# One layer of a hybrid trunk on one core: norm and gate stage in one block, the attention loop of TensorE written out, the order of two emptyings changed in the final stage

## The chip, the core and the metric

The kernel runs on one core of a Trainium2 chip. The metric is the device time of one execution in microseconds (us); a time given for a kernel is the median of several executions.

## What is computed

One decoder layer runs for a prompt of 1024 tokens and a sample group of 8 x 8 tokens, 1088 tokens (`NT`) in all, in float32. Cut to what matters here:

```
xn = RMSNorm_pre(x);  z = xn @ w_in                      (1024 -> 13312 columns)
A: dilated windowed softmax attention, 3 groups x 4 heads -> 512
B: HGRN2, 8 heads, 128 x 128 state                        -> 1024
C: causal pooling over 2, 4, 8, 16 positions              -> 512
gates = sigmoid(mg)                                       (mg: 3 x 1024 columns of z)
merged = gates_0*(y_a @ w_br_a) + gates_1*(y_b @ w_br_b) + gates_2*(y_c @ w_br_c)
x_next = x + RMSNorm_post(merged @ w_out)
```

## The kernel before

Each matrix is held as a sum of a rounded part ("hi", type fp32r) and a remainder ("lo"), and a product is three matmuls: hi x hi, lo x hi, hi x lo. Features lie on the partitions and tokens on the free axis; a projection of 128 columns (a "unit", `Conveyor.project`, L233 for its matmuls) runs in three chunks of 384, 384 and 320 tokens, one PSUM bank each. `Conveyor.load` (L200, SyncE's queue) brings raw weights, `Conveyor.split` (L207, L209, GpSimd) makes their hi and lo parts, `Conveyor.empty` (L246, L247, ScalarE) copies a bank out and frees it. Every engine has its own list of instructions in program order, written by hand, with semaphores between them; there is no planner. A stage is a block (`nc.Block`), and engines meet at its end.

The stages in order: `norm_phase` (normalise, transpose through TensorE, split x into `x_hi` and `x_lo`; the first unit runs in between), `gate_phase`, `attention_phase`, `hgrn_phase`, `pool_phase`, `final_phase`.

**Gate stage** (L478 to L763). Unit 1 is projected first, then ten pairs (`PAIRS`) of 128 gate columns go by a seven-product scheme: the 1024 features and the 1088 tokens are halved, and seven products r = 0 to 6 of 512 features by 544 tokens replace eight (L639, each in two pieces j of 272 tokens and 24 matmuls). Products 0, 3 and 5 take a plain quarter of x; products 1, 2, 4 and 6 take a combination of quarters: t1 = x12 - x11, t2 = x22 - t1, t3 = x22 - x12 and t4 = x21 - t2, where x11 to x22 are hi plus lo of a quarter. VectorE makes the quarters' sums and most differences (L705, L731 to L738), GpSimd two of these (L583, L586), ScalarE rounds them (`round_t`, L655) and the remainders are taken by VectorE (L710) and once by GpSimd (L592). The weights need four sums per pair (`w_sums`, VectorE, L727), and GpSimd splits the seven weight blocks of a pair (L578, L580) into a ring of four slots. Products run in the order 0 to 6. ScalarE copies products 0, 1 and 2 out (L652), VectorE adds them to products 3, 4 and 5 (L748, L754, L760), ScalarE takes the sigmoid and issues the store (L689, L693). Unit 1's banks are emptied by ScalarE between the roundings, and TensorE's first product waits until all three are empty.

**Attention stage**. TensorE runs four heads in a loop, `with pe.Fori(0, AH) as h` (L1833); so do the other engines, each with a loop of its own. A head ends with the next head's unit 0 and begins with its unit 1.

**Final stage** (L765 to L1172). Eight units of branch B (`U_B + t`) run with `y_hi`, `y_lo`; meanwhile the eight 128-row tiles of branches A and C are loaded one per t (`ac_stage`), rounded by ScalarE (`split_ac`, L1019) and their remainders taken by VectorE (L1096); TensorE waits for all eight (`acl_ready`) before the A and C units. Then t = 0 to 7 runs a unit of A (`u_a(t)`) and one of C (`u_c(t)`), four feature tiles each. ScalarE's list per t is:

```
for t in range(KO):
    if t > 0:
        act.wait_ge(ml_ready, t)          # y_lo of t-1 is made (VectorE L1116)
    empty u_a(t) into pb[0], c = 0, 1, 2
    if t < LAST:
        empty u_c(t) into pb[1], c = 0, 1, 2
        act.wait_ge(m_ready, t + 1)       # merged tile t (VectorE L1111, L1114)
        y_hi[t] = round(pb[1])            # L1047
```

A unit's chunk c can start only when the unit before has had its bank c emptied, so `u_c(t)` waits for the emptying of `u_a(t)`.

## Time and profile before

| | us |
|---|---|
| median of 3 runs (lowest, highest) | 1954.68 (1951.04, 1956.36) |
| the profiled execution | 1951.46 |
| its span, first to last instruction | 1949.6 |
| TensorE busy in it | 1868.6 (96%) |
| VectorE, ScalarE, GpSimd busy | 825.0, 385.1, 546.6 |
| mean granted TensorE clock | 0.988 of full speed |

PE is TensorE's matmul side, DVE VectorE, ACT ScalarE, POOL GpSimd, SP SyncE. Ends of matmuls are modelled, so their durations overlap; the spacing of the starts is the rate. "[14.47 <-X]" means 14.47 us idle before the instruction, ended by X. Times in the rows count from the span's start.

### The profile page before, as it was taken

To read this page: it belongs to the slowest core of one execution; us is meant where nothing else is said; L and a number is where in the kernel's file an instruction comes from. 1 tells how busy PE (TensorE), PEld (TensorE's weight loads), DVE (VectorE), ACT (ScalarE), POOL (GpSimd) and SP (SyncE) were. 2 spreads that over 40 slices of the span, in tenths; PEclk is the share of its full clock that TensorE was granted. 3 is DMA by queue.
4 is the path that set the end of the run, shared out by engine and by line. 5 is a ranking of instruction groups with operands and counts; after the bars stand their busy time and mean duration, and the time that the engine had idled before them with its cause. 6 is when DMAs were issued, how large, how long until landed. Compare 5 with 4: busy or idle time off the path is not lost. (4 is left out here: it accounts for less than half of the span.)

```text
span 1949.6 us, 34834 instructions
## 1 busy us (share of the span) xinstructions
PE 1868.6 (96%) x13888; PEld 1793.8 (92%) x13888; DVE 825.0 (42%) x1380; ACT 385.1 (20%) x922; POOL 546.6 (28%) x371
## 2 busy tenths in 40 slices
PE   7599999999999999999999999999999998989898
PEld 6599999989998999999999999999999998988897
DVE  7532321231232133113255675566466384446623
ACT  5222221310211221022011111101101112222321
POOL 2676662211221221221222221222212232344200
PEclk9799999999999999999999999999999999999999
DMA  5132324142233324314212112112202224555522
GB/s 163 55 111 92 112 91 124 52 107 76 72 63 112 95 53 105 103 48 97 84 45 67 35 53 67 44 54 67 67 22 68 67 91 164 181 196 175 158 96 87
DMA packets 245179, 176.31 MB, mean 90 GB/s; under 512 B 35789, under 2 KB 226637, under 8 KB 245068
## 3 DMA queue, kind: packets, MB, share of 16 engines
q1 hardware_dynamic: 205036, 132.51, 23.9%
q10 hardware_dynamic: 40032, 42.15, 6.3%
q8 instruction: 90, 1.47, 0.3%
q14 instruction: 21, 0.17, 0.0%
HBM read 131.83 MB, written 42.79 MB: 90 GB/s over the span
## 5 line engine op out<-in xcount | busy, mean ns | idle before, releaser
L233 PE MATMUL psum<-x_hi,w_hi 128*128 128x384 f32 (+1 forms) x2208 | 732.4, 336 | 24.6 <-ACT c_ext L247 10.4
L233 PE MATMUL psum<-x_lo,w_hi 128*128 128x384 f32 (+1 forms) x2208 | 714.9, 328 | 7.0 <-issue 7.0
L233 PEld LDWEIGHTS psum<-x_hi,w_hi 128*128 128x128 f32 x2208 | 418.3, 189 | 47.9 <-issue 33.8
L207 POOL CAST w_hi<-w_raw 128x1024 fp32r<-128x1024 f32 (+1 forms) x108 | 114.9, 1064 | 1187.9 <-PE psum L233 915.1
L233 PEld LDWEIGHTS psum<-x_lo,w_hi 128*128 128x128 f32 x2208 | 418.9, 190 | 0.0
L233 PE MATMUL psum<-x_hi,w_lo 128*128 128x384 f32 (+1 forms) x2208 | 412.2, 326 | 0.0
L233 PEld LDWEIGHTS psum<-x_hi,w_lo 128*128 128x128 f32 x2208 | 370.7, 188 | 0.0
L209 POOL TENSOR_TENSOR w_lo<-w_raw,w_hi 128x1024 fp32r<-128x1024 f32 (+1 forms) x108 | 258.5, 2393 | 8.6
L2044 ACT ACTIVATE a_feature<-psum 128x384 f32<-128x384 f32 (+1 forms) x100 | 45.2, 452 | 368.3 <-PE psum L233 363.4
L2156 DVE TENSOR_TENSOR a_prob<-psum,band 128x128 f32<-128x128 f32 (+1 forms) x64 | 21.5, 378 | 216.9 <-PE psum L1850 215.6
L639 PE MATMUL psum<-g_sum_hi,w_hi 128*128 128x272 f32 x320 | 85.6, 294 | 7.6 <-POOL w_hi L578 7.6
L639 PE MATMUL psum<-g_sum_lo,w_hi 128*128 128x272 f32 x320 | 85.0, 293 | 0.0
L639 PE MATMUL psum<-x_hi,w_hi 128*128 128x272 f32 x240 | 63.3, 291 | 14.5 <-ACT a_feature L247 14.5
L580 POOL TENSOR_TENSOR w_lo<-g_tmp,w_hi 128x512 fp32r<-128x512 f32 x55 | 74.2, 1350 | 4.4
L639 PEld LDWEIGHTS psum<-g_sum_hi,w_hi 128*128 128x128 f32 x320 | 62.2, 194 | 7.9 <-issue 7.9
L233 PE MATMUL psum<-m_y_hi,w_hi 128*128 128x384 f32 (+1 forms) x192 | 62.2, 328 | 2.4 <-DVE m_y_lo L1088 2.4
L1362 PEld LDWEIGHTS psum<-b_q_decayed,b_k_decayed 128*64 128x64 f32 x1584 | 51.3, 138 | 13.0 <-issue 8.4
L639 PE MATMUL psum<-x_lo,w_hi 128*128 128x272 f32 x240 | 63.2, 291 | 0.0
L233 PE MATMUL psum<-m_y_lo,w_hi 128*128 128x384 f32 (+1 forms) x192 | 62.4, 330 | 0.0
L639 PEld LDWEIGHTS psum<-g_sum_lo,w_hi 128*128 128x128 f32 x320 | 62.0, 194 | 0.0
L748 DVE TENSOR_TENSOR g_tmp<-psum,g_tmp 128x272 f32<-128x272 f32 x20 | 8.8, 442 | 124.3 <-PE psum L639 124.3
L639 PEld LDWEIGHTS psum<-x_hi,w_hi 128*128 128x128 f32 x240 | 46.2, 193 | 14.7 <-ACT a_feature L247 14.7
(275 smaller groups left out, 2582.5 us busy)
## 6 DMA issues: line engine op xcount, KB each, us to landing
w_raw<-in_w_in SPq DMA_DIRECT2D x94, 512.0 KB, 3.9
gate_rows<-g_tmp ACTq DMA_DIRECT2D x20, 544.0 KB, 2.9
s_cached<-in_cache_kv_w SPq DMA_DIRECT2D x128, 64.0 KB, 2.5
s_cached<-in_cache_kv_w SPq DMA_DIRECT2D x64, 128.0 KB, 2.4
spare<-branch_outputs SPq DMA_DIRECT2D x13, 544.0 KB, 6.2
a_feature<-group_weights SPq DMA_DIRECT2D x12, 512.0 KB, 5.0
c_gate<-gate_rows SPq DMA_DIRECT2D x11, 544.0 KB, 3.6
c_gate_raw<-gate_rows SPq DMA_DIRECT2D x11, 544.0 KB, 4.0
```

The lines of the kernel that those rows point to most:

```text
L207: pool.tensor_copy(w_hi[:, s, 0:nko, :], w_raw[:, s, 0:nko, :]).then_inc(self.hi_ready, 1)
L209: pool.tensor_tensor(w_lo[:, s, 0:nko, :], w_raw[:, s, 0:nko, :], w_hi[:, s, 0:nko, :].bitcast(F32), ALU.subtract)\
L233: mm = pe.matmul(psum[:, c, 0:n], w[:, s, k, :], x[:, k, t0:t0 + n], start=step is first, stop=step is last)
L580: pool.tensor_tensor(ring(w_lo, m), source(n, r), ring(w_hi, m).bitcast(F32), ALU.subtract)\
L639: mm = pe.matmul(bank(n, r, j), w[:, a.start, b.start + k, :], piece(x, j)[:, k, :], start=(r in (0, 1, 3) and w is w_hi and x is hi and k ...
L748: dve.tensor_tensor(outs[0][:, j * N:(j + 1) * N], bank(n, 3, j), kept1[j], ALU.add)\
L1362: mm = pe.matmul(bank[r:r + HP, b * wq:(b + 1) * wq], kr[:, t0 + r:t0 + r + HP], second(q[:, t0 + r:t0 + r + HP], n), start=True, stop=True)
L2044: ins = act.activation(by_class(DST[j][:, 0:SEQ], g)[:, :, t0 // STEP[g]:end // STEP[g]], psum[:, c, 0:end - t0].rearrange("p (m r) -> p r ...
L2156: ins = dve.tensor_tensor(prob[:, a:a + w], ps_, mask, ALU.add)
```

## The change

The norm stage and the gate stage become one block. The sums and differences of x, of the first pair's weights and their remainders all go to VectorE, the roundings of the first pair's weights to ScalarE; GpSimd splits weights from the second pair on. The first pair's raw weights are loaded as soon as unit 1's are split. The products run in the order 0, 3, 1, 2, 5, 4, 6, so that two plain ones come first; within a product the matmuls with the remainder of x come last. Scratch tiles share the memory of the x rows, `g_pre` and `q0`. In attention TensorE's loop over the heads is a Python loop, so its instructions are written four times; the other engines keep their loops. In the final stage two tiles of A and C are brought at each of the first four t, and ScalarE empties `u_a(t + 1)` right after it rounds tile t, without waiting for that tile's remainder.

```diff
-        def norm_phase(then, q0):
-
-
+        def norm_and_gate_phase(first, then, q0):
...
+            ORDER = (0, 3, 1, 2, 5, 4, 6)
+            SHIFT = 66
...
+                area = sb("x_rows", (P, (TILES + 1) * D), F32, scope)
+                xt = area[:, :].rearrange("p (t d) -> p t d", d=D)
...
+                junk = q0[:, 0:D]
...
+                FULLS = {"x12": 1, "x11": 2, "t1": 3, "x22": 4, "t2": 5, "t3": 6, "x21": 7, "t4": 8}
...
+                def slot(m):
+
+                    return m % 4 if m < SHIFT else (m + 2) % 4
...
+                        sp.wait_ge(cv.split_done, 2 * SLOTS)
+                        for n in range(PAIRS):
+                            if n == 1:
+                                sp.wait_ge(t_full, FULLS["t4"])
+                            if n > 1:
+                                weights_ready(sp, 7 * (n - 1) - 1)
...
+                        for n in range(1, PAIRS):
+                            for r in ORDER:
+                                m = place(n, r)
+                                source_ready(pool, n, r)
+                                slot_free(pool, m)
+                                pool.tensor_copy(ring(w_hi, m), source(n, r)).then_inc(p_hi_ready, 1)
+                                high_ready(pool, m)
+                                pool.tensor_tensor(ring(w_lo, m), source(n, r), ring(w_hi, m).bitcast(F32), ALU.subtract)\
+                                    .then_inc(p_ready, 1)
...
+                        for n in range(PAIRS):
+                            for r in ORDER:
+                                m = place(n, r)
+                                hi, lo, ready = moving(r)
+                                if n == 0 and r == 0:
+                                    cv.emptied(pe, 1)
...
+                                    if r == 0 and n > 1:
+                                        pe.wait_ge(copied, 8 * (n - 2) + 7 + j)
+                                    elif r == 3 and n > 0:
+                                        pe.wait_ge(summed, 6 * (n - 1) + 1 + j)
+                                    elif r == 1 and n > 0:
+                                        pe.wait_ge(summed, 6 * (n - 1) + 3 + j)
+                                    elif r == 2:
+                                        pe.wait_ge(copied, 8 * n + 1 + j)
+                                    elif r == 5:
+                                        pe.wait_ge(copied, 8 * n + 3 + j)
+                                    elif r == 4:
+                                        pe.wait_ge(copied, 8 * n + 5 + j)
+                                    elif r == 6:
+                                        pe.wait_ge(summed, 6 * n + 5 + j)
...
+                                    steps = [(w_hi, hi, k) for k in range(HK)] + [(w_lo, hi, k) for k in range(HK)]
+                                    steps += [(w_hi, lo, k) for k in range(HK)]
...
+                        def round_t(n, full, src):
+                            act.wait_ge(t_full, FULLS[full])
+                            act.activation(t_hi[n][:, :, :], src, ACT.Copy).then_inc(t_hi_ready, 1)
+
+                        def round_w(r):
+                            m = place(0, r)
+                            source_ready(act, 0, r)
+                            slot_free(act, m)
+                            act.activation(ring(w_hi, m), source(0, r), ACT.Copy).then_inc(first_hi_ready, 1)
...
+                        cv.emptied(act, 0, 1)
+                        act.activation(q0[:, 0:t0], q0[:, 0:t0], ACT.Sigmoid).then_inc(closed, 1)
+                        cv.empty(act, 0, NCH - 1, q0, ACT.Sigmoid)
+                        round_w(0)
+                        round_w(3)
+                        cv.emptied(act, 0)
+                        act.wait_ge(closed, 1)
+                        act.dma_start(gates_d[0], q0[:, :]).then_inc(first_out, 16)
+                        act.wait_ge(first_out, 16)
+                        cv.empty(act, 1, 0, q0, ACT.Sigmoid)
+                        round_t(0, "t1", tmp[1])
+                        cv.empty(act, 1, 1, q0, ACT.Sigmoid)
+                        cv.empty(act, 1, 2, q0, ACT.Sigmoid)
+                        round_w(1)
+                        round_w(2)
+                        cv.emptied(act, 1)
+                        act.dma_start(gates_d[1], q0[:, :]).then_inc(first_out, 16)
+                        round_t(1, "t2", tmp[3])
+                        for j in range(2):
+                            copy(kept1[j], 0, 0, j)
+                        round_w(5)
+                        round_t(2, "t3", tmp[0])
+                        round_w(4)
+                        for j in range(2):
+                            copy(kept5[j], 0, 1, j)
+                        round_w(6)
+                        round_t(3, "t4", tmp[3])
...
+                        def whole(name, dst, a, b):
+                            dve.tensor_tensor(dst, quarter(x_hi, a, b).bitcast(F32), quarter(x_lo, a, b).bitcast(F32),
+                                              ALU.add).then_inc(t_full, 1)
+
+                        def differ(name, dst, x, y, needs):
+                            dve.wait_ge(t_full, FULLS[needs])
+                            dve.tensor_tensor(dst, x, y, ALU.subtract).then_inc(t_full, 1)
+
+                        def low(n, src):
+                            dve.wait_ge(t_hi_ready, n + 1)
+                            dve.tensor_tensor(t_lo[n][:, :, :], src, t_hi[n][:, :, :].bitcast(F32), ALU.subtract)\
+                                .then_inc(t_ready[n], 1)
+
+                        def low_w(r):
+                            m = place(0, r)
+                            high_ready(dve, m)
+                            dve.tensor_tensor(ring(w_lo, m), source(0, r), ring(w_hi, m).bitcast(F32), ALU.subtract)\
+                                .then_inc(first_ready, 1)
...
+                        w_sums(0, (0, 1))
+                        dve.wait_ge(xt_done, 2 * (TILES + 1))
+                        dve.wait_ge(banks_free, 2 * (TILES + 1))
+                        whole("x12", tmp[0], 0, 1)
+                        whole("x11", tmp[1], 0, 0)
+                        w_sums(0, (2,))
+                        differ("t1", tmp[1], tmp[0], tmp[1], "x11")
+                        low_w(0)
+                        low_w(3)
+                        whole("x22", tmp[2], 1, 1)
+                        low(0, tmp[1])
+                        differ("t2", tmp[3], tmp[2], tmp[1], "x22")
+                        low_w(1)
+                        low_w(2)
+                        differ("t3", tmp[0], tmp[2], tmp[0], "x22")
+                        low(1, tmp[3])
+                        dve.wait_ge(t_full, FULLS["t3"])
+                        dve.wait_ge(t_full, FULLS["t2"])
+                        whole("x21", tmp[2], 1, 0)
+                        w_sums(0, (3,))
+                        low_w(5)
+                        dve.wait_ge(t_ready[1], 1)
+                        differ("t4", tmp[3], tmp[2], tmp[3], "x21")
+                        low(2, tmp[0])
+                        low_w(4)
+                        low(3, tmp[3])
+                        low_w(6)
+                        dve.wait_ge(t_ready[2], 1)
...
+                        for n in range(PAIRS):
+                            if n > 0:
+                                dve.wait_ge(out[0], 16 * n)
+                            for j in range(2):
+                                product_done(dve, n, 3, j)
+                                dve.wait_ge(copied, 8 * n + 1 + j)
+                                dve.tensor_tensor(outs[0][:, j * N:(j + 1) * N], bank(n, 3, j), kept1[j], ALU.add)\
+                                    .then_inc(summed, 1)
+                            if n + 1 < PAIRS and n > 0:
+                                w_sums(n + 1)
+                            for j in range(2):
+                                product_done(dve, n, 5, j)
+                                dve.wait_ge(copied, 8 * n + 5 + j)
+                                dve.tensor_tensor(outs[0][:, HN + j * N:HN + (j + 1) * N], bank(n, 5, j), kept2[j], ALU.add)\
+                                    .then_inc(summed, 1)
+                            if n > 0:
+                                dve.wait_ge(out[1], 16 * n)
+                            for j in range(2):
+                                product_done(dve, n, 4, j)
+                                dve.tensor_tensor(outs[1][:, HN + j * N:HN + (j + 1) * N], bank(n, 4, j), kept5[j], ALU.add)\
+                                    .then_inc(summed, 1)
+                            if n == 0:
+                                w_sums(1)
...
                         weights(U_B + 1)
                         sp.wait_ge(yl_ready, KO)
                         for t in range(KO):
-                            if t >= 3:
-                                sp.wait_ge(acl_ready, t - 2)
-                            sp.dma_start(ac_stage[t % 3][:, :], y_d[Y_A + t]).then_inc(ac_in[t % 3], 16)
+                            for k in (2 * t, 2 * t + 1) if t < KO // 2 else ():
+                                if k >= 3:
+                                    sp.wait_ge(acl_ready, k - 2)
+                                sp.dma_start(ac_stage[k % 3][:, :], y_d[Y_A + k]).then_inc(ac_in[k % 3], 16)
                             weights(U_B + t + 2)
...
                                 act.wait_ge(rows_out[t % 2], 16 * (t // 2))
                             for c in range(NCH):
                                 cv.empty(act, U_B + t, c, pb[t % 2], ACT.Copy)
-                            split_ac(t)
+                            for k in (2 * t, 2 * t + 1) if t < KO // 2 else ():
+                                split_ac(k)
                             act.wait_ge(gated, t + 1)
                             act.dma_start(merged_d[t], pb[t % 2][:, :]).then_inc(rows_out[t % 2], 16)
                         for r in range(2):
                             act.wait_ge(rows_out[r], 16 * (KO // 2))
-                        for t in range(KO):
+                        for c in range(NCH):
+                            cv.empty(act, u_a(0), c, pb[0], ACT.Copy)
+                        for t in range(LAST):
                             if t > 0:
                                 act.wait_ge(ml_ready, t)
                             for c in range(NCH):
-                                cv.empty(act, u_a(t), c, pb[0], ACT.Copy)
-                            if t < LAST:
-                                for c in range(NCH):
-                                    cv.empty(act, u_c(t), c, pb[1], ACT.Copy)
-                                act.wait_ge(m_ready, t + 1)
-                                act.activation(y_hi[:, t, :], pb[1][:, :], ACT.Copy).then_inc(mh_ready, 1)
+                                cv.empty(act, u_c(t), c, pb[1], ACT.Copy)
+                            act.wait_ge(m_ready, t + 1)
+                            act.activation(y_hi[:, t, :], pb[1][:, :], ACT.Copy).then_inc(mh_ready, 1)
+                            for c in range(NCH):
+                                cv.empty(act, u_a(t + 1), c, pb[0], ACT.Copy)
                         for c, (t0, n) in enumerate(CHUNKS):
                             act.wait_ge(m_ready, LAST + c + 1)
                             act.activation(y_hi[:, LAST, t0:t0 + n], pb[1][:, t0:t0 + n], ACT.Copy).then_inc(mh_ready, 1)
...
                             if t > 1:
                                 dve.wait_ge(gate_in[t % 2], 16 * (t // 2))
                             dve.tensor_tensor(pb[t % 2][:, :], pb[t % 2][:, :], gt[t % 2][:, :], ALU.mult).then_inc(gated, 1)
-                            dve.wait_ge(ach_ready, t + 1)
-                            dve.tensor_tensor(x_lo[:, t, :], ac_stage[t % 3][:, :], x_hi[:, t, :].bitcast(F32),
-                                              ALU.subtract).then_inc(acl_ready, 1)
+                            for k in (2 * t, 2 * t + 1) if t < KO // 2 else ():
+                                dve.wait_ge(ach_ready, k + 1)
+                                dve.tensor_tensor(x_lo[:, k, :], ac_stage[k % 3][:, :], x_hi[:, k, :].bitcast(F32),
+                                                  ALU.subtract).then_inc(acl_ready, 1)
...
-                        with pe.Fori(0, AH) as h:
+                        for h in range(AH):
...
-            norm_phase(first_of((COL_MG + D + 2 * P, COL_MG + D + 3 * P)), q0)
-            gate_phase(first_of((COL_AQ, COL_AK)), q0)
+            norm_and_gate_phase(first_of((COL_MG + D + 2 * P, COL_MG + D + 3 * P)), first_of((COL_AQ, COL_AK)), q0)
```

## Rows read from the trace of the kernel before

**Rows 1.** Waits of TensorE, longest in total: total us, times, longest

```profile
PE psum L233 <- ACT c_ext L247: 10.4, 7, 1.9
PE psum L639 <- POOL w_hi L578: 7.6, 2, 5.1
PE psum L233 <- issue: 7.0, 3, 2.4
PE psum L233 <- DVE x_lo L1096: 4.2, 1, 4.2
```

**Rows 2.** Timeline of TensorE, gate stage: start us, us, instruction, idle before

```profile
39.60 0.41 PE L233 MATMUL psum<-x_hi,w_hi 128*128 128x384 f32 x1 [0.47 <-PEq L359]
...
66.14 0.59 PE L639 MATMUL psum<-x_hi,w_hi 128*128 128x272 f32 x1 [14.47 <-ACT a_feature L247]
...
88.32 0.29 PE L639 MATMUL psum<-x_hi,w_hi 128*128 128x272 f32 x1
...
100.36 0.29 PE L639 MATMUL psum<-x_hi,w_hi 128*128 128x272 f32 x1
```

**Rows 3.** Timeline of VectorE and GpSimd, end of norm and start of gate stage

```profile
31.56 3.13 DVE L434 TENSOR_TENSOR x_lo<-psum,x_hi 128x512 fp32r<-128x512 f32 x6
...
49.09 2.42 DVE L705 TENSOR_TENSOR g_tmp<-x_hi,x_lo 128x2176 f32<-128x2176 f32 x1
...
74.25 0.69 DVE L727 TENSOR_TENSOR g_tmp<-w_raw 128x512 f32<-128x512 f32 x1
...
51.60 7.00 POOL L586 TENSOR_TENSOR g_tmp<-g_tmp 128x2176 f32<-128x2176 f32 x1 [7.29 <-DVE g_tmp L705]
```

**Rows 4.** Timeline of ScalarE, norm stage and start of gate stage

```profile
10.80 1.06 ACT L407 ACTIVATE x_hi<-psum 128x512 fp32r<-128x512 f32 x2
...
61.46 2.02 ACT L655 ACTIVATE g_sum_hi<-g_tmp 128x2176 fp32r<-128x2176 f32 x1 [9.97 <-DVE g_tmp L735]
63.39 0.47 ACT L247 ACTIVATE a_feature<-psum 128x384 f32<-128x384 f32 x1
...
71.59 0.66 ACT L652 ACTIVATE g_tmp<-psum 128x272 f32<-128x272 f32 x2
```

**Rows 5.** DMA issues, 0 to 60 us: KB each, median us to landing

```profile
gate_rows<-a_feature ACTq DMA_DIRECT2D x1, 544.0 KB, 4.5
```

**Rows 6.** The page's costliest groups: count, busy us, mean ns, idle before

```profile
L748 DVE TENSOR_TENSOR g_tmp<-psum,g_tmp 128x272 f32<-128x272 f32 x20 | 8.8, 442 | 124.3 <-PE psum L639 124.3
```

**Rows 7.** Busy time by stretch: us, PE, PEld, DVE, ACT, POOL, PEclk, DMA, GB/s

```profile
466.00:469.00 3.00, 3.00 (x11) 3.00 (x10) 0.00 (x0) 0.00 (x0) 0.00 (x0) 0.50 0.77 224
...
1732.00:1736.00 4.00, 3.37 (x11) 3.37 (x12) 0.58 (x1) 0.00 (x0) 0.00 (x0) 0.57 0.94 380
```

**Rows 8.** Timeline of TensorE, attention: first matmuls of heads 1, 2 and 3

```profile
303.04 0.43 PE L233 MATMUL psum<-x_hi,w_hi 128*128 128x384 f32 x1 [1.44 <-PEq L129]
...
462.98 0.44 PE L233 MATMUL psum<-x_hi,w_hi 128*128 128x384 f32 x1 [1.43 <-POOL w_hi L207]
465.75 0.33 PE L233 MATMUL psum<-x_lo,w_hi 128*128 128x384 f32 x1 [2.33 <-issue]
...
626.77 0.43 PE L233 MATMUL psum<-x_hi,w_hi 128*128 128x384 f32 x1 [0.99 <-ACT s_q L2055]
```

**Rows 9.** DMA queues, 303 to 463 us, then 1100 to 1552: packets, MB, share

```profile
q8 instruction: 11, 0.18, 0.5%
...
q8 instruction: 6, 0.10, 0.1%
```

**Rows 10.** Timeline of the final stage: ACT and DVE of t = 1, PE

```profile
1764.49 1.11 ACT L1047 ACTIVATE m_y_hi<-c_ext 128x1088 fp32r<-128x1088 f32 x1 [3.77 <-DVE c_ext L1114]
...
1765.63 1.29 DVE L1116 TENSOR_TENSOR m_y_lo<-c_ext,m_y_hi 128x1088 fp32r<-128x1088 f32 x1 [1.18 <-ACT m_y_hi L1047]
...
1767.59 0.41 PE L233 MATMUL psum<-x_hi,w_hi 128*128 128x384 f32 x1 [1.42 <-ACT c_ext L247]
...
1835.15 0.41 PE L233 MATMUL psum<-x_hi,w_hi 128*128 128x384 f32 x1 [1.42 <-ACT c_ext L247]
```

More of the change, by code:

```diff
@@ new lines, in slot, with previous, ring, block_of @@
+                def slot(m):
+                    return m % 4 if m < SHIFT else (m + 2) % 4
+                def previous(m):
+                    return max(i for i in range(m) if slot(i) == slot(m))
+                def ring(w, m):
+                    g = slot(m)
+                    return w[:, g // 2, g % 2 * HK:g % 2 * HK + HK, :]
+                def block_of(n, u, half):
+                    return raw[n % 2][:, u, half * HK:(half + 1) * HK, :]
+                def source(n, r):
+                    return (block_of(n, 0, 0), sums[0], sums[1], block_of(n, 0, 1), sums[2], sums[3], block_of(n, 1, 1))[r]
```

456 lines of the change are left out of this document (165 added, 291 removed).

## The prediction

> **What bounds the kernel now.** I read the table first: TensorE is busy 96% of the span, and VectorE, ScalarE and GpSimd less than half. So a gain can only come from stretches in which TensorE stands still or runs at half clock. Next, TensorE's waits, longest first [rows 1]; the longest of all, 14.47 us, stands in the timeline [rows 2]. Then the timeline at each of these places. Three stretches carry nearly all of them, and the change touches each. First, the start of the gate stage: after unit 1 TensorE waits 14.47 us for ScalarE, then 7.6 us in two pieces for split weights. Second, the turns of the attention loop, where the three "issue" waits of 7.0 us are. Third, the A and C units of the final stage: 4.2 us before them and 10.4 us in seven gaps between them.
>
> **Gate start.** Before, unit 1 starts at 39.60 and takes 66.14 - 14.47 - 39.60 = 12.07 us; the second pair starts at 100.36 [rows 2]. ScalarE's emptying of unit 1 stands in its queue behind the rounding of t3, which comes from a GpSimd difference of 7.00 us; the same size on VectorE, undisturbed, is 2.42 [rows 3].
>
> After, I follow the lists. There is no block end, so unit 1 runs from 39.13 (39.60 less its 0.47 idle) to 51.2; ScalarE's last emptying (0.47) [rows 4] lets the first product start at 51.7. ScalarE has by then waited for its store of unit 0, 4.5 us [rows 5], which ends before t1 exists and so is hidden by VectorE's list. The raw weights need only unit 1's split, long past, and land beside the norm's end.
>
> VectorE is free at 31.56 + 3.13 = 34.7. Its list is 2.42 us for each operation on a quarter and 0.69 for each on 512 columns (the sums, and I take it for the remainders too) [rows 3]. GpSimd has nothing to do meanwhile. Two sums, x12, x11, one sum, t1, two remainders, x22, low(0), t2, two remainders, t3, low(1), x21 and the fourth sum are nine of 2.42 and eight of 0.69: 27.3, so the fourth sum is ready at 62.0.
>
> TensorE: four products of 88.32 to 100.36 take 12.04, so 3.01 each [rows 2]. Products 0, 3, 1, 2 run from 51.7 to 63.7 without a stop: low(0) and low(1) are made at 50.2 and 58.9, before products 1 and 2 need them. Then new waits come. Product 5 needs the bank that product 1 left, and ScalarE copies it only behind `round_w(5)`, which waits for the fourth sum at 62.0. ScalarE's 512 columns cost half of 1.06 and its roundings of t 2.02, a copy 0.33 to 0.4 [rows 4]: 62.0 + 0.53 + 2.02 + 0.53 + 0.4 = 65.5, so TensorE idles 1.8. Product 5 ends at 68.5. Product 4 needs the copy of product 2, which stands behind `round_w(6)` and `round_t(3)`: 65.5 + 0.4 + 0.53 + 2.02 + 0.4 = 68.9, 0.4 idle; it ends at 71.9. Product 6 needs product 4 added up, and VectorE first ends its list: 62.0 + 0.53 (ScalarE) + 0.69 + t4 2.42 + low(2) 2.42 + 0.69 + low(3) 2.42 + 0.69 = 71.8, then five additions of 0.44 [rows 6]: 74.0, 2.1 idle. It ends at 77.0, where the second pair can start if its weights are there: their load waits for t4 (65.6) and GpSimd is free, so they are. Before, this was at 100.36: a gain of 23.4.
>
> Two costs are not in that. Hand-overs between engines, some ten in VectorE's and ScalarE's chain: I take 0.5. And the clock: after the 2.33 us wait at 465.75 TensorE ran at 0.50 of its clock, that is at 1.2 of its 2.4 GHz, for 3 us, 1.5 us lost [rows 7, 8]; after the 1.42 us gap at 1767.59 nothing shows, as the period below says [rows 10]. The waits of 1.8 and 2.1 lie between: 0, 1.5 or 3.0 us, and I take 1.5, since 2.1 is nearest to the 2.33. Gain 21.4, between 18 and 24.
>
> The trace shows what a wait in a list does to the rest: a bank whose unit had long run on was emptied only at 63.39, right behind a rounding that had waited 9.97 us [rows 4]. The Trainium skill says it as a rule ("TensorE: Matmul & The Clock Gate", architectural detail on engine queues): ScalarE and VectorE take their queues strictly in order. It speaks against this part of the change, and the trace agrees. By it the three new idles stand, 4.3 us; were the copies free to pass, the gain would be 4.3 larger.
>
> In the other nine pairs the same work stands in another order; GpSimd's splits, VectorE's sums and additions all had room (0.442 us per addition after long idles [rows 6]), and each bank is free one product earlier than it is asked for. I cost it at 0; what hides it is that only TensorE is full there. The Exp for the lower bound now stands at the stage's end, beside attention's unit 0: 0.
>
> **Attention.** The first pass starts at 303.04 and its last matmul ends at 462.98 - 1.43 = 461.55, 158.5 us later; the second pass is 626.77 - 462.98 = 163.8 from start to start [rows 8]. So one turn costs 5.3: a gap of about 1.2, the 2.33 "issue" after the first matmul, and 1.5 at half clock. Within a pass there is no such wait. The turn costs because the instructions are fetched: 11 blocks come in one pass of this loop, while HGRN's loop, nearly three times as long in the window, draws 6 in all [rows 9], and TensorE's list of waits has none at its turns. Written out, the same stream comes in order, as in the first pass. Nothing else ends late at the turn: the bank and the weights that unit 1 asks for are done during unit 0. Three turns: 3 x 5.3 = 15.9. The other engines keep their loops; they turn while TensorE is in unit 0. Bounds: 3 x (2.33 + 1.5) = 11.5 if the first gap stays, 16.5 if the loop's exit gains too.
>
> **Final stage.** With the A and C tiles done by t = 3, VectorE's remainder at the end of B is gone: 4.2 us [rows 1], and the half clock behind it, 4.00 x 0.43 = 1.7 less what idles in that window, so 1.6 [rows 7]. What the doubled tiles cost in t = 0 to 3 is one more transfer, rounding and remainder per t, beside a unit of 12 us on TensorE: hidden. The weights on SyncE's queue stand behind the second tile's wait for VectorE, a few us into a unit, and are due a unit later.
>
> In the A and C units, the emptying of `u_a(t + 1)` no longer waits for VectorE's remainder of tile t: 1.29 of the 1.42 idle, 1.34 with its hand-over [rows 10]. The period is (1835.15 - 1767.59) / 5 = 13.51; six gaps give 6 x 1.34 = 8.0, the first (1.9, the longest in [rows 1]) 1.8. What is late next is VectorE's multiply and add of the merged tile, still in the chain, so a gain stops there. Sum 4.2 + 1.6 + 8.0 + 1.8 = 15.6; the weights of `u_a(1)` wait for the last merged store and now have 5.8 us less room, so I take 15, between 11 and 16.
>
> **Sum.** 21.4 + 15.9 + 15 = 52.3, against 1951.46: 1899.2. That execution was 3.2 below the median of the runs shown; I add half: **1901 us**. A difference of 0.3%, about 6 us, is what a measurement of this kernel tells from none.
>
> **Rivals.** (a) The head's turn is not fetching but the releasers that the rows name, weights and an emptying [rows 8]: attention gains nothing, 1917. Against it, "issue" follows the first matmul, with everything ready. 0.08. (b) The gate's first pair is a longer chain than I count: VectorE's 2.42 is of an undisturbed one, and each quarter operation late by 0.5 moves the end by six or seven; gain 12, 1910. 0.13. (c) The final stage turns to waiting for weights or merged rows, whose loads follow one another in SyncE's queue: gain 7, 1909. 0.07. (d) Slower: TensorE's stream is now some 44 blocks for the four heads, not re-entered, and if each block's fetch stopped it 2.33 us, as at a turn, that costs 44 x 2.33 = 103: 2004. It decides from 22 stalled blocks on. Against it, the first pass reads its blocks in order with no wait. 0.02.
>
> **Numbers.** My forecast has 0.70. It runs from 1893 (all upper ends, less the medians' spread) to 1906; (b) and (c) need 1912, and (a) stays out. Faster 0.97, within 0.3% 0.01, slower 0.02.
>
> **What would show it.** Unit 1 followed by a product within 1 us; idles of about 2 us before products 5 and 6 of the first pair; the second pair near 78. Four equal passes of 158.5 us with no "issue" wait. No wait for L1096's successor, a period near 12.2 us in the A and C units. I am wrong if the second pair starts after 84, if a turn still shows a gap over 1 us, or if the period stays at 13.5.

## The result, and the profile after

The changed kernel takes **1893.22 us** (median of 4 runs, 1891.13 to 1895.16) against 1952.86 for the kernel before beside it: ratio 0.9693, interval 0.9672 to 0.9715. In a later comparison it gave 1891.77 and 0.9694 (0.9681 to 0.9708). The forecast was 1901 us, between 1893 and 1906. The direction and the three places were right; the gain is 59.6 us where 53.7 was forecast. The time lies 0.2 us inside the low end of the range, and that of the later comparison below it.

The page of the changed kernel, its span, the busy times and the queue that loads instructions (q8: blocks, MB, share):

```profile
span 1893.4 us, 34539 instructions
...
PE 1855.8 (98%) x13888; PEld 1783.4 (94%) x13888; DVE 825.3 (44%) x1390; ACT 388.4 (21%) x929; POOL 524.6 (28%) x354
...
q8 instruction: 80, 1.31, 0.3%
```

TensorE issues the same work and is busy 98% of a shorter span, where it was 96%. Its waits in the changed kernel, longest in total first (total us, times, longest; "issue", where it stands as the cause of a wait, is time in which the engine waited for nothing that the profile shows):

```profile
PE psum L524 <- DVE x_rows L684: 13.2, 5, 8.2
PE psum L233 <- PEq L129: 3.9, 2, 2.6
PE psum L233 <- DVE m_y_lo L1118: 2.4, 1, 2.4
PE psum L233 <- ACT c_ext L247: 2.0, 1, 2.0
PE psum L570 <- DVE x_rows L778: 1.7, 1, 1.7
...
PE psum L570 <- ACT x_rows L609: 0.5, 1, 0.5
PE psum L570 <- ACT a_feature L247: 0.5, 1, 0.5
```

Set beside [rows 1]: the 7.6 us for split weights, the three "issue" waits and the 4.2 us for VectorE have no successor; `c_ext` has one wait of 2.0 us where it had seven of together 10.4. Of the gate's products, L639 there and L570 here, which waited 14.47 and 7.6 us, 2.7 us of waits are left. The first line, the norm stage, is about as before (13.9 us there).

Where the time went, from TensorE's timelines of the two profiled executions (spans 1949.6 and 1893.4 us):

| stretch | before, us | after, us | gain | forecast |
|---|---|---|---|---|
| start to attention's first matmul | 303.04 | 278.02 | 25.0 | 21.4 |
| attention, first matmul to HGRN's first | 651.30 | 634.09 | 17.2 | 15.9 |
| HGRN, pool, to the first B unit | 680.26 | 680.43 | -0.2 | 0 |
| B, A and C units, to the output columns | 208.81 | 194.62 | 14.2 | 15 |
| the rest | 106.19 | 106.24 | 0.0 | 0 |

The bounds that are shown neither in [rows 8] nor below: HGRN's first matmul, the first B unit and the output columns before, then the last two after.

```profile
954.34 0.41 PE L233 MATMUL psum<-x_hi,w_hi 128*128 128x384 f32 x1 [1.14 <-ACT b_forget_new L247]
...
1634.60 0.45 PE L233 MATMUL psum<-m_y_hi,w_hi 128*128 128x384 f32 x1 [2.38 <-DVE m_y_lo L1088]
...
1843.41 0.39 PE L984 MATMUL psum<-w_hi,m_y_hi 128*128 128x256 f32 x1 [0.68 <-POOL w_lo L946]
...
1592.54 0.44 PE L233 MATMUL psum<-m_y_hi,w_hi 128*128 128x384 f32 x1 [2.38 <-DVE m_y_lo L1118]
...
1787.16 0.39 PE L1012 MATMUL psum<-w_hi,m_y_hi 128*128 128x256 f32 x1 [1.10 <-POOL w_lo L974]
```

The gains are 56.2 us. The medians differ by 59.6, because the profiled execution of after is the slowest of its four runs, and that of before (1951.46) lies below its median.

**Gate.** TensorE's timeline in the changed kernel (start us, us, instruction, idle before):

```profile
51.80 0.78 PE L570 MATMUL psum<-x_hi,w_hi 128*128 128x272 f32 x4 [0.53 <-ACT a_feature L247]
...
64.63 0.77 PE L570 MATMUL psum<-x_hi,w_hi 128*128 128x272 f32 x4 [0.53 <-ACT x_rows L609]
...
72.59 0.77 PE L570 MATMUL psum<-g_sum_hi,w_hi 128*128 128x272 f32 x4 [1.71 <-DVE x_rows L778]
...
75.69 0.67 PE L570 MATMUL psum<-x_hi,w_hi 128*128 128x272 f32 x4
```

These are product 0, product 5, product 6 and the second pair, which stood at 100.36 [rows 2]. Of these 24.7 us, 19.3 are waits (22.0 before the first pair's products then, 2.8 now) and 0.4 is the block's end. The other 5.0 are TensorE's clock: in the kernel before it was granted 0.52, 0.50 and 0.58 in the 4 us behind the three waits, and seven products took 26.65 us without their waits, against 21.65 now, at 1.00 throughout. VectorE's list in the same kernel, which sets the last of these waits:

```profile
55.84 2.42 DVE L707 TENSOR_TENSOR g_sum_lo<-x_rows,g_sum_hi 128x2176 fp32r<-128x2176 f32 x1
58.18 2.42 DVE L698 TENSOR_TENSOR x_rows<-x_hi,x_lo 128x2176 f32<-128x2176 f32 x1
60.51 0.68 DVE L728 TENSOR_TENSOR x_rows<-w_raw,g_pre 128x512 f32<-128x512 f32 x1
...
70.11 0.68 DVE L713 TENSOR_TENSOR w_lo<-w_raw,w_hi 128x512 fp32r<-128x512 f32 x1
70.72 0.78 DVE L765 TENSOR_TENSOR x_rows<-psum,x_rows 128x272 f32<-128x272 f32 x2
71.42 0.78 DVE L772 TENSOR_TENSOR x_rows<-psum,x_rows 128x272 f32<-128x272 f32 x2
```

Read starts, not durations: the first three follow each other by 2.34 and 2.33 us, though each whole operation (128x2176) lasts 2.42; a small one (128x512) is followed after 0.61, though it lasts 0.68; two additions take 0.70.

**Attention.** TensorE's first matmul of heads 0 and 1, and of HGRN:

```profile
278.02 0.41 PE L233 MATMUL psum<-x_hi,w_hi 128*128 128x384 f32 x1 [1.27 <-PEq L129]
...
436.30 0.34 PE L233 MATMUL psum<-x_hi,w_hi 128*128 128x384 f32 x1
...
912.11 0.41 PE L233 MATMUL psum<-x_hi,w_hi 128*128 128x384 f32 x1 [1.14 <-ACT b_forget_new L247]
```

Head 1 starts with no idle before it, where [rows 8] had 1.43 and, a matmul later, 2.33. Later heads start at 594.47 and 752.63, so a pass is 158.2 us.

**Final stage.** The chain that ended last, at the turn from B to the A and C units (start us, us, what):

```profile
1688.28 5.24 DMA merged_rows<-c_ext
...
1693.59 0.50 ACT c_ext L247
1694.09 0.14 issue
1694.22 90.45 PE psum L233 x540
```

From there to the output columns TensorE runs 540 matmuls without a stop; the seven gaps of [rows 1] are gone. One thing was not foreseen: ScalarE empties `u_a(0)` only when the last merged store, of 5.24 us, has landed, and TensorE idles 1.95 us for it at the next unit, the first C unit.

### The profile page after: what moved, and what is told of

Its sections match the earlier page's. It is cut to its first block and busy times, and to the rows that moved or that the text cites. A ratio compares the mean times of both kernels' runs of the same rounds, so it can differ in the third digit from the quotient of the medians.

```text
span 1893.4 us, 34539 instructions
## 1 busy us (share of the span) xinstructions
PE 1855.8 (98%) x13888; PEld 1783.4 (94%) x13888; DVE 825.3 (44%) x1390; ACT 388.4 (21%) x929; POOL 524.6 (28%) x354
## 5 line engine op out<-in xcount | busy, mean ns | idle before, releaser
L233 PEld LDWEIGHTS psum<-x_hi,w_hi 128*128 128x128 f32 x2208 | 415.9, 188 | 21.9 <-issue 16.3
L1538 DVE COPY_PREDICATED b_att<-b_level,psum 64x256 f32<-64x256 int32 (+2 forms) x136 | 58.8, 432 | 2.3
L1393 PE MATMUL psum<-b_q_decayed,b_k_decayed 128*64 128x32 f32 x1584 | 56.6, 224 | 0.7
L247 ACT ACTIVATE c_ext<-psum 128x384 f32<-128x384 f32 (+1 forms) x69 | 30.9, 471 | 118.0 <-PE psum L233 111.2
L570 PE MATMUL psum<-g_sum_hi,w_hi 128*128 128x272 f32 x320 | 53.2, 288 | 1.7 <-DVE x_rows L778 1.7
L570 PE MATMUL psum<-g_sum_lo,w_hi 128*128 128x272 f32 x320 | 52.8, 287 | 0.0
L570 PE MATMUL psum<-g_sum_hi,w_lo 128*128 128x272 f32 x320 | 52.8, 287 | 0.0
L609 ACT ACTIVATE x_rows<-psum 128x272 f32<-128x272 f32 x80 | 31.6, 398 | 101.7 <-PE psum L570 101.7
L570 PEld LDWEIGHTS psum<-g_sum_hi,w_hi 128*128 128x128 f32 x320 | 45.0, 188 | 1.9 <-DVE x_rows L778 1.9
L506 POOL TENSOR_TENSOR w_lo<-x_rows,w_hi 128x512 fp32r<-128x512 f32 x33 | 44.7, 1354 | 2.6
```

Of the source, the lines that this page charges most:

```text
L233: mm = pe.matmul(psum[:, c, 0:n], w[:, s, k, :], x[:, k, t0:t0 + n], start=step is first, stop=step is last)
L247: act.activation(dst[:, t0:t0 + n], psum[:, c, 0:n], func).then_inc(self.bank_free, 1)
L506: pool.tensor_tensor(ring(w_lo, m), source(n, r), ring(w_hi, m).bitcast(F32), ALU.subtract)\
L570: mm = pe.matmul(bank(n, r, j), ring(w, m)[:, k, :], piece(x, j)[:, k, :], start=(r in (0, 1, 3) and at == 0), stop=(at == len(steps) - 1) ...
L609: return act.activation(dst, bank(n, r, j), func).then_inc(copied, 1)
L1393: mm = pe.matmul(bank[r:r + HP, b * wq:(b + 1) * wq], kr[:, t0 + r:t0 + r + HP], second(q[:, t0 + r:t0 + r + HP], n), start=True, stop=True)
```

## The experiments

Each is an edit of the changed kernel unless it says otherwise, and compared in the trace with the second profile of the changed kernel (span 1889.6; attention from 277.92 to 912.04). Where a kernel has only one execution, the verdict is the place in the trace and not the total.

**1. The loop back in attention's TensorE part.**

```diff
-                        for h in range(AH):
+                        with pe.Fori(0, AH) as h:
```

> The changed kernel with TensorE's attention loop back; all else as changed. If the turn of that loop costs because its instructions are fetched again: three turns of 163.79 - 158.17 = 5.6 us come back, each with an issue wait of about 2.3 us after the first matmul of a head, so 16.9 us more than the changed kernel, about 1910. If the gaps belonged to the weights and the emptying that the rows named: nothing comes back, about 1893.

Measured 1911.75 us (1911.46 to 1913.72), ratio 0.979 (0.9773 to 0.9806): 18.5 above the changed kernel's 1893.22, 20 above its 1891.77. Attention takes 652.11 against 634.12, **18.0 more**. TensorE's timeline at the first turn of this kernel:

```profile
437.67 0.44 PE L233 MATMUL psum<-x_hi,w_hi 128*128 128x384 f32 x1 [1.31 <-POOL w_hi L207]
...
440.28 0.48 PE L233 MATMUL psum<-x_hi,w_hi 128*128 128x384 f32 x1 [1.99 <-issue]
440.56 0.52 PE L233 MATMUL psum<-x_lo,w_hi 128*128 128x384 f32 x1
```

The "issue" waits are back (1.99, 2.15, 2.19), and with each comes a stretch at half clock: 0.52 us for a matmul that takes 0.33 at full clock. So the loop, and nothing else of the change, made these waits. That the row names `w_hi` for the first gap misleads: GpSimd made that tile from 436.53 to 437.57 here and from 436.49 to 437.53 in the changed kernel, where TensorE started the same unit at 436.20 without it.

**2. One turn of four.** Two heads in a loop, two written out.

```diff
+                        with pe.Fori(0, 2) as h:
+                            head(h)
+                        head(2)
+                        head(3)
```

> Heads 0 and 1 in a loop of two passes, heads 2 and 3 written out: one turn in place of three. If the cost is one of the turn: 5.6 us more than the changed kernel, all at head 1's start, and no gap at the starts of heads 2 and 3. If it is a cost of having a loop at all, for instance of values in registers inside a pass: half of the 16.9, spread over the two passes.

One execution: attention 641.18, 7.1 more. The one turn shows gaps of 1.29 and 2.54 at 438.08 and 441.24, then half clock; TensorE's list of waits has no other of either kind. The price goes by turns. It is 7.1 here and 6.0 per turn in run 1, because the half clock differs: granted 0.81 from 437 to 455, so 3.4 us lost, against 3.4, 1.8 and 1.8 at the three turns of run 1.

**3. Make another loop too long.** HGRN's loop body on TensorE holds two heads instead of one; the work is the same.

```diff
-                        with pe.Fori(0, BH - 1) as i:
-                            head(i, ...)
+                        with pe.Fori(0, BH // 2 - 1) as g:
+                            head(g * 2, ...)
+                            head(g * 2 + 1, ...)
+                        head(BH - 2, ...)
```

> HGRN's loop on TensorE takes two heads per pass (three passes, then two heads written out), so its body is twice as long, longer than attention's; nothing else differs from the changed kernel. If a turn costs when its body is too long to be still there: two turns inside the loop cost some 4 to 6 us each, 8 to 12 us more, with an issue wait after the first matmul of the pass, where the single-head loop shows none. If attention's turn had a cause of its own: no new gap in HGRN, and the time of the changed kernel.

One execution: HGRN and pool take 602.50 against 597.94, 4.6 more for two turns. The mechanism is confirmed, with a smaller price. TensorE's timeline at one of them:

```profile
1087.31 1.20 PE L1402 MATMUL psum<-ident,b_v_new 128*128 128x128 f32 x9 [1.30 <-ACT b_gate_new L247]
...
1091.87 0.69 PE L1393 MATMUL psum<-b_q_new,b_k_decayed 128*64 128x64 f32 x16 [0.55 <-issue]
```

and the queue that loads instructions, between the two turns (1095 to 1225 us; packets, MB, share):

```profile
q8 instruction: 11, 0.18, 0.6%
```

With one head in the body, the same stretch of the changed kernel loads no instruction block at all. So a body of 631 matmuls, as the profile counts them, is kept and its turn is free; 1262, or attention's 1097, is loaded anew in each pass. Where the limit lies between 631 and 1097 was not tried. HGRN's turn is cheaper since the second wait is 0.55 and 0.82 instead of 2 to 2.5, and the clock stays at 1.00.

**4. Norm and gate stage of before, the rest changed.**

> The norm and gate stages of before, with the changed attention and final stage. If the parts add up, the start of the gate stage costs what the two traces differ by at the second pair, 100.36 - 75.69 = 24.7 us, and 0.3 more by attention's start: about 25 us above the changed kernel, 1918. If part of that gain only replaced waits that come later anyway, less than 20.

Measured 1918.91 us (1918.63 to 1920.11), ratio 0.9828 (0.9812 to 0.9845). Attention starts at 303.52, 25.6 later. Three parts, then: 18.0 of run 1, 25.6 of this run and, from the table, 14.2 of the final stage make 57.8, between the 56.2 of the two profiles and the 59.6 of the medians. They add: attention takes 634.19 here, and starts at 277.80 in run 1, as in the changed kernel.

**5. The final stage's tiles one per step, as before.** ScalarE's and SyncE's loops are edited alike.

```diff
-                            for k in (2 * t, 2 * t + 1) if t < KO // 2 else ():
+                            for k in (t,):
```

> The changed kernel with the A and C tiles loaded one per t again. If the landing of the last merged store is what limits the changed kernel there: TensorE waits 4.2 us for the last remainder and loses 1.6 us at half clock, but the 1.95 us gap before the first C unit falls away, so 3.9 us more. If the terms simply add: 5.8 us more.

Measured 1898.31 us (1895.57 to 1899.65), ratio 0.9718 (0.9704 to 0.9733). The wait for VectorE is back, with half clock behind it, and no gap between the units. TensorE's timeline:

```profile
1690.49 0.69 PE L233 MATMUL psum<-x_hi,w_hi 128*128 128x384 f32 x1 [4.24 <-DVE x_lo L1127]
```

The stretch is 197.85 against 194.13, only 3.7 longer, since this wait covers the 1.96 us for the store.

**6. ScalarE's order in the A and C units as before.**

```diff
-                        for c in range(NCH):
-                            cv.empty(act, u_a(0), c, pb[0], ACT.Copy)
-                        for t in range(LAST):
+                        for t in range(KO):
                             if t > 0:
                                 act.wait_ge(ml_ready, t)
+                            for c in range(NCH):
+                                cv.empty(act, u_a(t), c, pb[0], ACT.Copy)
...
-                            for c in range(NCH):
-                                cv.empty(act, u_a(t + 1), c, pb[0], ACT.Copy)
```

> The changed kernel with ScalarE's old order in the A and C units. If the remainder of each tile was what the emptying waited for: seven gaps of 1.42 us and their slow starts come back, 10 to 11 us more, about 1904. If the chain through the merged tile sets the period anyway: no more than 3 us.

Measured 1904.11 us (1903.86 to 1905.3), ratio 0.9752 (0.9737 to 0.9767). All seven gaps are back, behind the wait for the store. TensorE's timeline, the first three of the eight:

```profile
1691.15 0.41 PE L233 MATMUL psum<-x_hi,w_hi 128*128 128x384 f32 x1 [1.99 <-ACT c_ext L247]
...
1705.17 0.41 PE L233 MATMUL psum<-x_hi,w_hi 128*128 128x384 f32 x1 [1.93 <-ACT c_ext L247]
...
1720.29 0.41 PE L233 MATMUL psum<-x_hi,w_hi 128*128 128x384 f32 x1 [1.42 <-ACT c_ext L247]
```

The stretch is 12.7 longer: 12.4 us of such waits less the 2.0 of the changed kernel, a half-clock stretch behind the gap at 1705 (granted 0.67 and 0.90 in the 8 us after it, about 1.7 lost), and 0.6 that has no place. The order is worth more than three times what the tiles are beside the wait for the store.

**7. The third difference (t3) on GpSimd again, within the new stage.**

```diff
-                        differ("t3", tmp[0], tmp[2], tmp[0], "x22")
...
+                        pool.wait_ge(t_full, FULLS["t2"])
+                        pool.tensor_tensor(tmp[0], tmp[2], tmp[0], ALU.subtract).then_inc(t_full, 1)
```

> The changed kernel with the difference t3 on GpSimd, which stands idle until 72 us, in place of VectorE. If the two engines slow each other on operations of this size, as the 7.00 us of the old GpSimd difference and the 7.15 us of the VectorE sum beside one suggest: the first pair ends no sooner, the second pair starts 0 to 3 us later than 75.7. If VectorE's list alone sets the end of the first pair: it is 2.3 us shorter, and the second pair starts 1.7 us sooner, all of the wait before product 6.

One execution: 2.4 us later at attention's start. Timelines of GpSimd and VectorE in this kernel:

```profile
52.19 4.89 POOL L500 TENSOR_TENSOR x_rows<-x_rows 128x2176 f32<-128x2176 f32 x1 [26.52 <-DVE x_rows L705]
...
52.28 5.95 DVE L715 TENSOR_TENSOR w_lo<-g_pre,w_hi 128x512 fp32r<-128x512 f32 x2 [0.17 <-ACT w_hi L621]
```

Beside GpSimd's 4.89 us, two remainders of VectorE take 5.95 instead of 1.29. Alone it is the first that is late: it lasts 5.35 us, 0.55 beyond the end of GpSimd's operation, and the second takes its usual 0.68 behind it. VectorE gives its 2.33 us away and loses 4.66 in its place. Its later list shifts by 2.4, product 5 waits 2.85 us, and half clock follows.

**8. One remainder (low(3)) made twice**, into the same tile, which lengthens VectorE's list by one operation.

> The changed kernel with the remainder of t4 made twice, one more VectorE operation of 2.34 us in the list that product 6 of the first pair waits for. If the list sets that wait: it grows from 1.7 to about 4.1 us. If TensorE's clock falls in a wait of that length, as before the A and C units of the kernel before (4.24 us, then 0.57): 1.5 more is lost, and the second pair starts 3.9 us later, at 79.6. If the clock stays: 2.4 us later, at 78.1.

One execution: product 6 starts at 75.27 instead of 72.53, 2.7 later, and attention at 282.20, 4.3 later; the rest is the clock. VectorE's list is what product 6 waits for. Busy times of 74 to 78 and 78 to 82 us in this kernel (PE, PEld, DVE, ACT, POOL, then the granted clock, DMA, GB/s):

```profile
74.00:78.00 4.00, 2.73 (x13) 2.73 (x14) 3.97 (x8) 1.77 (x2) 3.31 (x4) 0.71 0.91 244
78.00:82.00 4.00, 4.00 (x30) 4.00 (x29) 2.47 (x2) 1.13 (x3) 3.60 (x4) 0.86 0.60 226
```

**9. ScalarE waits for each merged store only ahead of the unit that uses its buffer.**

```diff
-                        for r in range(2):
-                            act.wait_ge(rows_out[r], 16 * (KO // 2))
+                        act.wait_ge(rows_out[0], 16 * (KO // 2))
                         for c in range(NCH):
                             cv.empty(act, u_a(0), c, pb[0], ACT.Copy)
+                        act.wait_ge(rows_out[1], 16 * (KO // 2))
```

> The changed kernel, but ScalarE waits for the last store of each merged buffer only before it overwrites that buffer: the even one before it empties the first A unit, the odd one before the first C unit. If the new 1.95 us gap before the first C unit is the landing of the last merged store: it goes, about 2 us less than the changed kernel, and nothing takes its place, as the next weights land some 1.5 us before they are asked for. If the weights that wait for the same store are next: the gap moves to the second A unit, and nothing is gained.

Measured 1892.36 us (1889.72 to 1894.17), ratio 0.9687 (0.9674 to 0.9701). The wait of 1.95 is gone; what is left is 0.18 us at a later unit, for weights. The stretch is 193.84 with a half-clock start of B, and 192.21 in run 10, which has the same edit and no such start: 1.9 less than 194.13. In the total nothing can be told from the changed kernel.

**10. The same, and ScalarE's copies of products 1 and 2 ahead of its roundings in the gate.**

```diff
+                        for j in range(2):
+                            copy(kept5[j], 0, 1, j)
                         round_w(5)
                         round_t(2, "t3", tmp[0])
                         round_w(4)
-                        for j in range(2):
-                            copy(kept5[j], 0, 1, j)
                         round_w(6)
+                        for j in range(2):
+                            copy(kept2[j], 0, 2, j)
                         round_t(3, "t4", tmp[3])
```

> The own-buffer kernel, with ScalarE's copies of products 1 and 2 of the first pair set ahead of the roundings that wait for VectorE. If VectorE's list sets the end of the first pair: the 0.53 us wait before product 5 goes, the wait before product 6 grows by as much, and the second pair starts where it did, 75.7. If the strict order of ScalarE's list were what holds TensorE: 0.5 to 1 us sooner.

One execution. Product 5 no longer waits, but product 4 then waits 0.52 us for its split weights, and product 6 1.90 us for VectorE: it starts at 72.89, no sooner. Behind the 1.90 us TensorE went to half clock, where behind 1.71 us in the changed kernel it did not; attention starts at 279.81, 1.9 later. Busy times of 74 to 78 us, first in the changed kernel (its second profile):

```profile
74.00:78.00 4.00, 4.00 (x34) 4.00 (x33) 3.93 (x4) 1.53 (x4) 3.84 (x4) 1.00 1.04 353
```

and in this one:

```profile
74.00:78.00 4.00, 4.00 (x22) 4.00 (x21) 3.93 (x4) 1.45 (x3) 3.84 (x5) 0.57 0.89 279
```

**11. Run 9 and, in the first pair alone, VectorE's additions of product 4 ahead of those of products 3 and 5.** The waits that count these additions are renumbered to match.

```diff
+                        for j in range(2):
+                            product_done(dve, 0, 4, j)
+                            dve.wait_ge(copied, 3 + j)
+                            dve.tensor_tensor(outs[1][:, HN + j * N:HN + (j + 1) * N], bank(0, 4, j), kept5[j], ALU.add)\
+                                .then_inc(summed, 1)
                         for n in range(PAIRS):
...
-                            for j in range(2):
+                            for j in range(2) if n > 0 else ():
                                 product_done(dve, n, 4, j)
```

> Two edits to the changed kernel: ScalarE waits for the last merged store only ahead of the unit that uses its buffer, and in the gate's first pair VectorE adds up product 4 ahead of products 3 and 5. If what holds product 6 back is VectorE's list as it stands (four additions of 0.35 us start to start between its last remainder and product 4's addition), product 6 starts 0.45 us behind product 4's end instead of 1.7, so near 71.3, TensorE's clock stays full, and the second pair starts near 74.4 instead of 75.6; attention starts 1.2 earlier. Rival: product 6 or the second pair then waits for something else (the remainder of the fourth sum, the second pair's weights, split by GpSimd from 71.9 on), and the second pair stays at 75.6. With the 1.9 us that the wait at the final stage's first unit costs, the whole is near 3 us below the changed kernel (1888 to 1890), under what a measurement tells, so the verdict is the places in the trace.

Measured 1890.93 us (1888.15 to 1892.56), ratio 0.9677 (0.9664 to 0.9691). TensorE's timeline, product 6 and the second pair:

```profile
71.01 0.77 PE L570 MATMUL psum<-g_sum_hi,w_hi 128*128 128x272 f32 x4 [0.32 <-DVE x_rows L762]
...
74.10 0.67 PE L570 MATMUL psum<-x_hi,w_hi 128*128 128x272 f32 x4
```

Product 6 waits 0.32 us instead of 1.71, the second pair starts 1.5 sooner, attention at 276.40, 1.5 sooner; B to the output columns takes 192.32, 1.8 less than 194.13. Both places moved as expected. They make 3.3 us; the medians differ by 0.8 to 2.3, and the intervals overlap, so a faster total is not shown.

## What the prediction had right, and the step that failed

**What bounds the kernel** was read rightly: all of the gain lies in stretches where TensorE stood or ran at half clock, and stages outside the three changed by 0.2 us. The mechanisms were right in all three places. What failed is the size of two terms, gate start (25.0 us measured, bounds 18 to 24) and attention (17.2, bounds 11.5 to 16.5).

**Gate start: right in mechanism, 3.6 us too small** (21.4 forecast). The step that failed is the price of VectorE's list: durations of back-to-back operations were added, 2.42, 0.69 and 0.44, where start to start is 2.33, about 0.61 and 0.35. Up to product 6 the list has twelve whole operations, eleven small ones and five additions, so 1.0 + 0.7 + 0.4 = 2.1 us were counted too much. The Trainium skill says why ("Perfetto Trace Analysis", on the per-engine timelines): for VectorE the reported window runs until the write is acknowledged, and the next instruction may begin before that. The trace agrees, with 2.42 beside 2.33. Hence the waits were 0.53 before product 5 (1.8 forecast), none before product 4 (0.4), 1.71 before product 6 (2.1), and the second pair came at 75.7, not 77.0.

The second term that was off is the 1.5 us for one half-clock stretch: the clock stayed at 1.00. The forecast had rows for a wait of 1.42 us and one of 2.33 and chose between them. In all eight profiles with a wait of 1.68 to 1.72 us before product 6 the clock stayed; run 10, with 1.90 there, paid the price. The 0.5 for hand-overs is about what came: 0.28 before the remainders for products 1 and 2, 0.18 before that for product 5, 0.05 before product 6. The list also began 0.2 later than counted, and product 6 took 3.10, not 3.0. So 2.1 + 1.5 - 0.2 - 0.1 = 3.3 of the 3.6; the last 0.3 are gained in the nine later pairs and the stage's end. Run 8 shows VectorE's list as what sets the end, run 11 which part of it could go, and run 7 that the difference had to leave GpSimd, as [rows 3] let one think. Rival (b), a longer chain than counted, was the wrong way round.

**Attention: right in mechanism, 1.3 us too small**: 17.2 measured, 15.9 forecast, no "issue" wait. "The turn costs because the instructions are fetched" holds in runs 1 to 3; rival (a) falls with the result and with run 1, rival (d) with the absence of any stall across the four heads. The Trainium skill has this too ("Runtime: NRT & Kernel Launch", Instruction fetch mechanics): a taken branch whose target lies outside the current window of two blocks must load it before going on, and straight code is loaded ahead. The trace agrees on both, but not on the two blocks: HGRN's body has over half of the matmuls of attention's, which loads 10 or 11 blocks in a pass, and turns without loading one. The runs give the price, 6.0 us per turn in run 1 (18.0 / 3). The term was undersized by its own reading: the pass was measured to the end of its last matmul, 158.5, but matmuls overlap, and from start to start it is 158.2. That is 0.34 in each of three turns, 1.0; the last 0.3 has no measured place.

**Final stage: the sum nearly right (14.2 against 15), its parts less so.** The tiles' 4.2 + 1.6 and the gaps are gone as forecast, and the gaps wholly: 10.4, where 8.0 + 1.8 = 9.8 were counted. What the step "the weights of `u_a(1)` wait for the last merged store" looked for came at ScalarE instead: it waits for that same store before it empties `u_a(0)`, which costs TensorE 1.95 us. This wait was there in the code, hidden under the 4.24 us for VectorE (run 5), and the question what is late next was put to the gaps only. Rival (c) is half right, then: not the weights, but a store, and at a quarter of the 8 us that it would have cost (run 9). With 0.4 more at the output columns (1.1 for split weights, 0.7 before), 16.2 - 2.0 - 0.4 = 13.8 of the 14.2 are placed. So the sum came out near the forecast in part by luck: 0.6 had been taken off for late weights, and the store took 2.0.

**The sum.** By the stages 56.2 us against 52.3; 3.6 of the difference is the gate. The half of 3.2 us added because the profiled run lay below its median went the wrong way: after's median is 1.9 below its own profiled run. The low end of the range, 1893, had every term at its upper bound, and two of the three measured terms lie above theirs. The spread between the two profiles of the changed kernel, 3.8 us, has a place: the first unit of the final stage, behind a wait of 2.6 us, ran at half clock in one (granted 0.57 in the 4 us behind it) and at full clock in the other, and B's first unit, which then waited 2.38 or 0.86 us for VectorE, started 18.50 or 15.41 us after it.

**The signs named**: the second pair within 84, no turn with a gap, the A and C units without a pause, at a period of 12.04 where 12.2 was forecast: all came. Two idles "of about 2 us" before products 5 and 6 were 0.5 and 1.7.

## What to carry to other kernels

Where an engine works through a list without a stop, take its price from the starts of neighbouring rows, not from their durations; the same goes for a pass of matmuls. A loop whose body is too long to be kept is paid at every turn, which shows as an "issue" wait that ends 2.6 to 4.9 us behind its first instruction (runs 1 to 3) and as blocks in the instruction queue; look at that queue before writing a loop out, because a body that is kept turns free. When a wait is removed, list every other wait of the instruction that follows it: a shorter one that it covered comes out, as the store did here.

## What was not expected of the hardware

- The length of a wait alone did not decide whether TensorE's clock fell. It stayed at 1.00 behind 1.71 us (product 6) and behind 1.95 us (before the first C unit), and halved behind 1.90 (run 10). Behind 1.93 us it halved in run 6 and stayed at 1.00 in the kernel before, at the same place, the first of the seven gaps; behind a wait of 2.6 us the same kernel did the one and the other. Before the first C unit it also halved in runs 3 and 4, where the wait was 2.05 and 2.15. What decides is open.
- Beside each other, GpSimd and VectorE did not share the time of these operations: one stood until the other was done. Two sums of the kernel before start together:

```profile
39.43 4.88 POOL L583 TENSOR_TENSOR g_tmp<-x_hi,x_lo 128x2176 f32<-128x2176 f32 x1 [14.04 <-POOLq L359]
39.45 7.15 DVE L705 TENSOR_TENSOR g_tmp<-x_hi,x_lo 128x2176 f32<-128x2176 f32 x1 [3.33 <-PEq L359]
```

VectorE's ends 2.29 us after GpSimd's, its own 2.33 start to start. The 7.00 us of GpSimd in [rows 3] began 0.05 after an operation of VectorE of 2.43 us, and ended 4.62 after it. In run 7 GpSimd began first and took 4.89, and VectorE's remainder ended 0.55 after it. That a small operation can so stand behind a long one of the other engine is what run 7 lost.

- A turn's price differs by loop: about 6.0 us in attention (18.0 for three) and 2.3 in the doubled HGRN loop (4.6 for two), with about the same number of instruction blocks, 10 or 11 in a pass. In attention 3.5 of it are the two waits and most of the rest is the half clock behind them; HGRN's turn kept its clock. Why its second wait is shorter was not tried.
